# Score products of the recurrent heads as 128x32 stationary tiles instead of 128x128 ones

## The reference, cut to what matters

```python
def step(state, inp):                       # one chunk of tokens
    qc, kc, vc, gc = inp
    bcum = jnp.cumsum(gc, axis=-2)
    b_ref = bcum[..., mid:mid + 1, :]
    inter = jnp.einsum('bhck,bhkv->bhcv', qc * jnp.exp(bcum), state)
    scores = jnp.einsum('bhtk,bhsk->bhts', qc * jnp.exp(bcum - b_ref), kc * jnp.exp(b_ref - bcum))
    intra = jnp.einsum('bhts,bhsv->bhtv', jnp.where(mask, scores, 0.0), vc)
    new_state = (jnp.exp(b_end[..., 0, :])[..., None] * state
                 + jnp.einsum('bhsk,bhsv->bhkv', kc * jnp.exp(b_end - bcum), vc))
    return new_state, inter + intra
...
o_f, _ = _chunk_gla(q, kf, v, gf, sc_f)
o_b, _ = _chunk_gla_rev(q, kb, v, gb, sc_b)
y = _hgrn_readout(o_f + o_b, gate, norm_g, w_out)
```

## Time and profile before

| what | value |
|---|---|
| executions, median of 3 | 4814.28 us (4812.27 to 4815.09) |
| span of the profiled execution | 4811.0 us; the median lies 3.3 us above it |
| TensorE matmul busy | 4415.6 us, 92% of the span |
| VectorE, ScalarE busy | 2549.0 us, 1634.9 us |
| mean granted TensorE clock | 0.959 of full speed |
| score products (L2427) | 1024 records, 1916.5 to 2653.3 us |

### The profile page before, as it was taken

How to read it: one execution, slowest core, us unless ns; L and a number is a source line. 1 busy time by engine, 2 the same in 40 slices (tenths; PEclk the granted TensorE clock), 3 DMA queues, 4 the chain that set the end, 5 groups by cost and what they waited for, 6 DMA issues and landing times. The chain is left out here.

```text
span 4811.0 us, 79247 instructions
## 1 busy us (share of the span) xinstructions
PE 4415.6 (92%) x32172; PEld 3347.7 (70%) x32172; DVE 2549.0 (53%) x3995; ACT 1634.9 (34%) x2499; POOL 443.6 (9%) x403
## 2 busy tenths in 40 slices
PE   8898999999999988999998899978998999899987
PEld 7665787675788767888887744456877567666675
DVE  3634543433434333888887369943534355454553
ACT  2324321323322232666665211133222233333332
POOL 0120000000000000222222000000000022121220
PEclk9888999999999999999999999989999999999998
DMA  3201222221122232111111221211221210000101
GB/s 144 106 19 70 88 105 92 88 88 53 70 105 88 107 124 82 47 58 46 58 49 38 109 84 70 88 53 70 104 97 71 104 37 20 21 20 20 52 6 53
DMA packets 36639, 337.16 MB, mean 70 GB/s; under 512 B 4080, under 2 KB 6384, under 8 KB 18544
## 3 DMA queue, kind: packets, MB, share of 16 engines
q1 hardware_dynamic: 36336, 332.76, 18.6%
HBM read 320.16 MB, written 12.58 MB: 69 GB/s over the span
## 5 line engine op out<-in xcount | busy, mean ns | idle before, releaser
L539 PE MATMUL ps<-hi,weight_parts 128*128 128x512 f32 x5136 | 1611.1, 394 | 120.9 <-DVE lo L406 76.0
L539 PEld LDWEIGHTS ps<-hi,weight_parts 128*128 128x128 f32 x5136 | 979.3, 191 | 341.7 <-issue 122.5
L539 PE MATMUL ps<-lo,weight_parts 128*128 128x512 f32 x2568 | 1011.4, 394 | 0.0
L527 DVE TENSOR_TENSOR weight_parts<-w,weight_parts 128x1024 fp32r<-128x1024 f32 (+1 forms) x336 | 407.0, 1213 | 968.0 <-ACT weight_parts L518 967.9
L518 ACT ACTIVATE weight_parts<-w 128x1024 fp32r<-128x1024 f32 (+1 forms) x336 | 351.7, 1048 | 1197.5 <-PE ps L539 996.6
L539 PEld LDWEIGHTS ps<-lo,weight_parts 128*128 128x128 f32 x2568 | 490.1, 191 | 102.0
L3501 PEld LDWEIGHTS ps<-buffers 64*64 64x64 f32 x12544 | 431.1, 136 | 140.5 <-issue 138.7
L3501 PE MATMUL ps<-buffers 64*64 64x64 f32 x12544 | 460.5, 225 | 67.1 <-issue 41.3
L2402 PE MATMUL ps<-x_parts,column_parts 128*128 128x512 f32 x1536 | 364.9, 395 | 9.9 <-DVE column_parts L2628 9.9
L2402 PEld LDWEIGHTS ps<-x_parts,column_parts 128*128 128x128 f32 x1536 | 287.6, 189 | 75.2 <-DVE column_parts L2628 10.3
L2858 PE MATMUL ps<-x,w 128*128 128x512 f32 x768 | 332.3, 596 | 5.2 <-PEq L815 5.2
(11 more groups left out here) (490 smaller groups left out, 5729.3 us busy)
## 6 DMA issues: line engine op xcount, KB each, us to landing
w<-in_weights SPq DMA_DIRECT2D x126, 2048.0 KB, 7.6
w<-in_wh SPq DMA_DIRECT2D x64, 512.0 KB, 3.6
v_kept<-buffers SPq DMA_DIRECT2D x4, 1024.0 KB, 5.2
buffers<-v_kept SPq DMA_DIRECT2D x16, 256.0 KB, 2.6
h<-x_kept SPq DMA_DIRECT2D x2, 2048.0 KB, 10.3
x<-in_xT SPq DMA_DIRECT2D x4, 512.0 KB, 10.8
x_kept<-h SPq DMA_DIRECT2D x1, 2048.0 KB, 6.8
vc_kept<-x SPq DMA_DIRECT2D x4, 512.0 KB, 2.6
```

Of the source, the lines that this page charges most:

```text
L527: dve.tensor_tensor(K.parts[:, j % 2, 1, 0:nk, :], part_of(K, slot, j, nk, by_row), K.parts[:, j % 2, 0, 0:nk, :].bitcast(F32), ALU.subtra ...
L539: mm = pe.matmul(ps, K.parts[:, j % 2, m, k, :], x[:, k * T:(k + 1) * T], start=(first and k == 0 and n == 0), stop=(last and k == nk - 1 ...
```

## The change

`scores` no longer computes 128x128 products. A new generator `score_tiles` lists, for a direction and a kind, the pieces of one block as (first key, first query, number of queries), always with 32 keys. Each piece is a product with a 128x32 stationary tile whose result lands on the 32 PSUM partitions of its keys.

```diff
+            def score_tiles(d, kind):
+
+                if kind < 2:
+                    for a in range(0, P, 32):
+                        q = a + 16 * (1 - d) if kind else a
+                        yield a, q, 16 if kind else 32
+                else:
+                    z = 16 << (kind - 1)
+                    for a in range(0, P, 2 * z):
+                        keys, queries = (a, a + z) if d == 0 else (a + z, a)
+                        for m in range(0, z, 32):
+                            yield keys + m, queries, z
+
             def scores(p, d, kind):
                 bank = K.ps[:, 4 + kind % 2, :]
+                l, r = (DK, DQ) if kind == 0 else (LV[:, (kind - 1) * T:kind * T],) * 2
                 for i in range(TT):
-                    s = slice(i * P, (i + 1) * P)
-                    l, r = (DK, DQ) if kind == 0 else (LV[:, (kind - 1) * T:kind * T],) * 2
-                    mm = pe.matmul(bank[:, s], l[:, s], r[:, s], start=True, stop=True)
+                    for a, q, n in score_tiles(d, kind):
+                        keys, queries = slice(i * P + a, i * P + a + 32), slice(i * P + q, i * P + q + n)
+                        mm = pe.matmul(bank[a:a + 32, queries], l[:, keys], r[:, queries], start=True, stop=True,
+                                       skip_group_check=True)
                 mm.then_inc(PR.step(f"sc{kind}{d}"), 1)
```

## The result

The changed kernel takes 4834.19 us, median of four executions (4829.92 to 4837.36), beside 4814.68 us for the kernel before (4812.27 to 4815.73). The ratio is 1.0044 with a 95% interval of 1.0032 to 1.0056: slower by 0.4%, where the prediction took 0.2% as what can't be told from none, and 14 us above its range. The profiled span is 4827.7 us against 4811.0.

The account below looks back on a forecast made before the run. TensorE bounds the kernel until VectorE's masked copies bind in the scores. Gains of 0.28 (d = 0) and 0.49 us (d = 1), 0.77 a head over fifteen heads, make 11.5: span 4799.5, with 3.3 around it 4803 us; range 4794 to 4820.

Parts of the forecast that it names:

- t's range: In the scores, the time per small-tile record of kinds 0 and 1: 0.008 to 0.029 us, taken as 0.016.
- the floor for kind 3: In the scores, kind 3 may load only 0.05 us after VectorE's second masked copy, `m1`, ends.
- the three first kinds: In the scores, kinds 0, 1 and 2 were to earn nothing but waiting for VectorE's masked copies.
- Kind 3 with its switch: End of the scores: 0.45 plus 0.26 us to `cs`, which comes 0.28 (d = 0) and 0.49 us (d = 1) earlier.
- One head: One head was to take 46.85 us instead of 47.62, a gain of 0.77.
- The last head: The head without projections, partly at half clock: between -2 and +2 us, taken as 0.
- The pace: Kinds 0 and 1 of the scores: about 1.1 us instead of 1.78, at 0.016 us a record.
- Rival 1: Score records issue slowly: 4804 us at 0.025 us a record, 4810 at 0.029; chance 16%.
- Rival 3: Small score tiles take turns, column groups not overlapping: 4822 us with loads hidden, 4848 half hidden, about 4890 not hidden; chance 12%.
- Rival 2: Emptier scores let TensorE's clock fall, 3.1 us a fall: 4818 us for one head in three, 4849 every head; chance 14%.
- the clock shows 0.50 within the heads: Sign of being wrong: TensorE's clock at 0.50 (1.2 GHz) within the heads, where 1.00 was forecast from 2000 to 2590.

Follow-up runs that it names:

- e13_after_prepad: The changed kernel with 32 needless products (128 instructions) executed once ahead of TensorE's loop: 4792.57 us, ratio 0.9952 to the kernel before.
- e1_kinds23: The changed kernel with kinds 0 and 1 computed as before, only kinds 2 and 3 in small tiles: 4797.56 us, ratio 0.9965 to the kernel before.
- e2_unrolled_after: The changed kernel with TensorE's loop written out as sixteen straight steps: 4805.96 us, ratio 0.9983 to the kernel before.
- e7_kinds123: The changed kernel with kind 0 computed as before, kinds 1, 2 and 3 in small tiles: 4788.24 us, ratio 0.9952 to the kernel before.
- e12_after_pad: The changed kernel with 32 needless products (128 instructions) executed once behind TensorE's loop: 4826.33 us, ratio 1.0027 to the kernel before.
- e8_kinds01: The changed kernel with kinds 2 and 3 computed as before, only kinds 0 and 1 in small tiles: 4810.06 us, ratio 0.9994 to the kernel before.
- e11_kinds23_pad: Only kinds 2 and 3 in small tiles, plus 128 needless instructions executed once behind the loop: 4787.74 us, ratio 0.9945 to the kernel before.

## Why the prediction was wrong

**The step that failed** is one sentence of the change part by part: "The extra 64 products per direction lengthen TensorE's instruction stream; its cost is bounded by t's range." (There are 32 more products per direction; 64 is their records, and with the weight loads 128 instructions.) It took the cost of an instruction to be its time to issue. The cost was in holding the loop: 512 more instructions in a pass, nine packets fetched each time, a jump back of 3.77 to 5.29 us instead of 0.21, and about 2 us more at half clock behind it. Six pairs in the loop take 595.3 us against 6 x 93.4 = 560.4, 34.9 more; 3.2 of them are another matter ("The clock"), and the other 31.7 go with the six jumps. No rival named it, and no row that I read could have priced it: the page of before shows q8 with 234 packets, and 1 in the 600 us of the change. But the count of instructions could be had from the diff, and the queue's line was in the page.

**What the tiles are worth** was right in mechanism. `m1` is the floor for kind 3, TensorE arrives first, and the three first kinds earn mostly waiting: in the changed kernel's list of waits from 2000 to 2600 L2441 now waits 19.3 us for L2690, 0.80 a direction in 24 directions, where 0.5 or more was forecast. Kind 3 with its switch takes 0.57 us (2341.22 to 2341.79) instead of the 0.71 taken, and `m1`'s end to `cs` 0.63 instead of 0.77. One head takes 46.7 us undisturbed instead of 46.85, that is 0.9 less than before where 0.77 was forecast. (The two directions' 0.14 would make it 1.05; the wait of the sum for ScalarE, 1.12 us where it was 0.94, would account for the difference.) `e13_after_prepad` has a stage 9.7 us shorter than the kernel before, beside 11.5 forecast; its first pair, at 96.6, costs 3.2 and keeps it below the forecast. The last head, given between -2 and +2 us, costs it 1.6: from that head's first `cs` to the end of the stage it takes 35.1 us, the kernel before 33.5. In d = 1 the slack of kind 2 over `m0` was missed, with no effect on the sum.

**The pace** was mis-sized. Kinds 0 and 1 need 0.70 us and not about 1.1. Their last record starts 0.57 us after the first, 0.009 us a record, near the lower bound of 0.008 and not the 0.016 taken. Rival 1 had the rule of the Trainium skill's page "TensorE: Matmul & The Clock Gate", section "Wait — 56ns, not 53.3ns?", of some 25 ns from start to start: across four column groups it didn't hold, in 64 records in a row. Rival 3 had its Part 3, section "The mechanism", by which a load overlaps a running matmul only where their row groups differ: it didn't hold either, for all these tiles use all rows. Either would have brought `cs` later than forecast, and it came earlier.

**The clock.** Rival 2 saw a fall, and it came in two places. In the steady heads the scores don't lower the clock: it is 1.00 in `e1_kinds23` and `e13_after_prepad` over the 600 us, with all their waits. In the changed kernel's 600 us it fell behind the jumps, after 5 us with 1.12 us of work, which is the thin stretch of the earlier trace rows over again. In the first head, ahead of that window, the scores did lower it. TensorE waits longer there, for GpSimd's factors and for VectorE's masked copy. `e13_after_prepad`, timeline, then windows:

```profile
1915.12 0.46 PE L2441 MATMUL ps<-h 128*32 128x32 f32 x32
1916.84 0.44 PE L2441 MATMUL ps<-h 128*32 128x16 f32 x32 [1.26 <-POOL h L2638]
...
1920.49 0.65 PE L2441 MATMUL ps<-h 128*32 128x32 f32 x16 [2.40 <-DVE w L2694]
```

```profile
1915.00:1920.30 5.30, 1.83 (x71) 1.34 (x70) 5.30 (x5) 1.90 (x4) 5.30 (x5) 1.00 0.02 5
1920.30:1930.50 10.20, 8.46 (x62) 7.87 (x63) 5.76 (x15) 3.97 (x6) 0.76 (x2) 0.50 0.16 53
```

That is rival 2 as it was told, at its price: one fall costs 3.2 us (96.6 against 93.4), where 3.1 was reckoned. `e2_unrolled_after`, `e7_kinds123`, the changed kernel and `e12_after_pad` have the same fall of 10.2 us in the first head; the kernel before and `e1_kinds23`, whose kinds 0 and 1 keep TensorE busier there, have none, and `e8_kinds01` has one of 3.4 us with no loss in its pair. Of the signs of being wrong, "the clock shows 0.50 within the heads" came true both ways.

**The sign.** The pauses hold 31.1 us of the stage (818.2 against 787.1), more than three times what the tiles bring. Without the pause the change is faster: 4792.57 with the pad ahead. Of the profiled execution's 18.4 us the stage gives 9.7 and the shifted code behind it another 7.1. The best versions run are `e11_kinds23_pad`, 4787.74 us, and `e7_kinds123`, 4788.24, and both beat both kernels. Of `e11_kinds23_pad`'s 27 us, the 14.8 of the stage (796.8 to 782.0) are the tiles'; of what is left, the 6.5 behind the stage are owed to the place of the code, and another edit may take them back.

## What to carry to other kernels

Count the instructions that a change adds to a hardware loop's body, weight loads included, before counting its time; if the instruction queue's packets jump from a few to some nine a pass, the loop no longer fits, and the cost is a pause at its top with a half-clock stretch behind it. The duration of the loop's branch, in the view of the loop's own line, says so directly. Take the part of a change that earns most for its instructions: kinds 2 and 3 brought 1.7 of 1.8 us a pair for a quarter of them. When a far stage moves by some microseconds after an edit that it doesn't contain, repeat the comparison with a pad of instructions executed once, and compare stage by stage.

## What the hardware showed that I had not expected

- A loop of TensorE holding 1700 instructions is fetched again on each pass or held, by where it begins: 54 packets and 98.6 to 101.0 us a pair, or 3 packets and 93.4 us, with the same loop 128 instructions on.
- The branch back takes 3.77 to 5.29 us where a held loop's takes 0.21, and TensorE's next 24 records then take 7.36 to 7.92 us instead of 5.63, at a granted clock of 0.50 for about 4 us.
- Emptier scores lowered the clock once, in the first head: 1.83 us of work in 5.30, then 10.2 us at 0.50 and 3.2 us lost.
- 64 records with 128x32 tiles over four column groups start 0.009 us apart, where one full-width record of 128 columns takes 0.111.
- 128 instructions executed once behind the loop make the kernel before 12 us faster (0.9976, 0.9966 to 0.9985), 7 of them in stages that they don't touch.
